# Scale column kept in idle norm columns; low parts of weight slots behind each quarter's sums; sums ahead of the odd chunk

## The reference: what is computed

```
c_act = jax.nn.silu(c)
mod = c_act @ ada_w[layer] + ada_b[layer]
sh_m, sc_m, g_m, sh_f, sc_f, g_f = jnp.split(mod, 6, axis=-1)
hm = x * (1.0 + sc_m) + sh_m
...
proj = (h @ w_in).astype(jnp.float32)
qa, ka, va, ra, aa, qkb, vb, ib, fb, ob = split_cols(proj, AB_SPLITS)
```

## Time and profile before

| | |
|---|---|
| median of 3 runs | 1407.68 us (1406.48 to 1409.59) |
| the profiled execution: its time, its span | 1406.98 us, 1405.2 us |
| mean granted TensorE clock | 0.981 |
| PE busy | 1343.3 us, 96% of the span |
| DVE, ACT, POOL busy | 619.5, 456.8, 507.5 us |

### The profile page before, as it was taken

One profiled execution on the slowest core, in us unless ns is written; L12 is line 12 of the kernel. 1 busy time (PEld: TensorE's weight loads), 2 busy tenths in 40 slices (PEclk: granted clock), 3 DMA queues, 4 the chain that ended last, 5 costly groups with the idle time before them and its releaser, 6 DMA issues.

```text
span 1405.2 us, 17072 instructions
## 1 busy us (share of the span) xinstructions
PE 1343.3 (96%) x6558; PEld 1111.4 (79%) x6558; DVE 619.5 (44%) x842; ACT 456.8 (33%) x622; POOL 507.5 (36%) x209
## 2 busy tenths in 40 slices
PE   7999999889999999999899999988989999999996
PEld 6778877778888888888788777878888888887885
DVE  4489657578534343300884323347692101100006
ACT  3343254333232332112322344316243323232112
POOL 0243222323453444344235122220254444444444
PEclk9999999999999999999999899999999999999998
DMA  9972546522555465643325421112023322234312
GB/s 332 165 150 80 190 135 121 180 76 98 191 190 195 163 218 173 183 129 96 119 80 191 113 90 53 42 57 76 30 91 108 101 91 103 90 103 137 90 60 60
DMA packets 93538, 173.81 MB, mean 124 GB/s; under 512 B 15736, under 2 KB 61960, under 8 KB 93357
## 3 DMA queue, kind: packets, MB, share of 16 engines
q1 hardware_dynamic: 90344, 169.63, 39.1%
q10 hardware_dynamic: 3140, 3.43, 0.9%
HBM read 170.87 MB, written 4.52 MB: 125 GB/s over the span
## 4 chain that ended last, share of the span: by engine, by line
PE 68%; issue 19%; POOL 6%; DVE 4%; ACT 1%; DMA 1%; SPq 0%; POOLq 0%; DVEq 0%; ACTq 0%
PE ps L1099 13%; PE ps L1100 13%; PE ps L1101 13%; POOL w_lo L692 6%; PE ps L1131 6%; PE ps L1132 6%; PE ps L1133 6%; PE ps L1614 1%; PE ps L1274 1%; PE ps L1275 1%; PE ps L1276 1%; PE ps L1642 1%; PE ps L1625 1%; PE ps L1629 1%; PE ps L1288 1%
## 5 line engine op out<-in xcount | busy, mean ns | idle before, releaser
L692 POOL TENSOR_TENSOR w_lo<-raw,w_hi 128x1024 fp32r<-128x1024 f32 x197 | 488.3, 2484 | 857.1 <-ACT w_hi L738 856.7
L1099 PE MATMUL ps<-h_lo,w_hi 128*128 128x512 f32 (+2 forms) x1064 | 402.0, 378 | 15.1 <-DVE h_lo L2138 5.9
L1100 PE MATMUL ps<-h_hi,w_hi 128*128 128x512 f32 (+2 forms) x1064 | 398.1, 374 | 0.0
L1101 PE MATMUL ps<-h_hi,w_lo 128*128 128x512 f32 (+2 forms) x1064 | 397.8, 374 | 0.0
L738 ACT ACTIVATE w_hi<-raw 128x1024 fp32r<-128x1024 f32 x203 | 213.2, 1057 | 483.9 <-PE ps L1133 177.0
L1099 PEld LDWEIGHTS ps<-h_lo,w_hi 128*128 128x128 f32 (+1 forms) x1064 | 203.8, 192 | 55.1 <-issue 8.4
L1101 PEld LDWEIGHTS ps<-h_hi,w_lo 128*128 128x128 f32 (+1 forms) x1064 | 203.7, 191 | 35.4
L1100 PEld LDWEIGHTS ps<-h_hi,w_hi 128*128 128x128 f32 (+1 forms) x1064 | 204.2, 192 | 34.2
L2235 DVE TENSOR_TENSOR tmp<-tmp,ps 128x512 f32<-128x512 f32 x44 | 30.1, 688 | 261.4 <-PE ps L1101 261.4
L1131 PE MATMUL ps<-w_hi,hid_lo 128*128 128x512 f32 x344 | 136.8, 398 | 1.8 <-issue 0.9
L1133 PE MATMUL ps<-w_lo,hid_hi 128*128 128x512 f32 x344 | 136.8, 398 | 0.0
(11 more groups left out here) (276 smaller groups left out, 1586.3 us busy)
## 6 DMA issues: line engine op xcount, KB each, us to landing
raw<-wstream SPq DMA_DIRECT2D x205, 512.0 KB, 4.0
ada_raw<-astream SPq DMA_DIRECT2D x80, 512.0 KB, 4.3
ada_first<-astream SPq DMA_DIRECT2D x16, 256.0 KB, 6.8
ada_first<-astream SPq DMA_DIRECT2D x8, 512.0 KB, 10.5
ln_rows<-row_scratch SPq DMA_DIRECT2D x3, 1024.0 KB, 6.7
skew_scratch<-f_scratch ACTq DMA_DIRECT2D x1, 2304.0 KB
xa<-xT SPq DMA_DIRECT2D x4, 512.0 KB, 8.5
out<-xa SPq DMA_DIRECT2D x3, 512.0 KB, 3.5
```

The lines of the kernel that those rows point to most:

```text
L692: nc.gpsimd.tensor_tensor(w_lo[:, slot, :], raw[:, slot % RAW, :], w_hi[:, slot, :].bitcast(F32), ALU.subtract).then_inc(sem("w_lo_ready"), 1)
L1099: pe.matmul(o, w_h, x_l, start=start, stop=False)
L1100: pe.matmul(o, w_h, x_h, start=False, stop=False)
L1101: return pe.matmul(o, w_l, x_h, start=False, stop=stop)
```

## The change

The place of `scale_b1` becomes the columns 0 to 7 of the sixth row of `cols`, which norms use only later; the arena begins 32 bytes lower. Row block 7 of quarter 3 goes from DVE to PE. On PE `first_cols(p + 1)` stands ahead of the odd chunk 2p + 1, for all three quarters that follow; before, it stood behind the first half of the odd chunk for p = 0 and 1, and ahead of chunk 5 for p = 2. On DVE, the low parts of slots 2, 3, 4 and 5 go behind all row blocks of the next quarter, and for p = 0 the low parts of chunk 0 and of slot 1 go ahead of the first row blocks of quarter 1.

```diff
-    scale_b1 = at("scale_b1", [P, KC])
...
+    scale_b1 = cols[:, 5, 0:KC]
...
-    FIRST_ON_PE = ((0, 1, 2, 3), (7,), (7,), ())
+    FIRST_ON_PE = ((0, 1, 2, 3), (7,), (7,), (7,))
...
         for p in range(4):
             for k in (2 * p, 2 * p + 1):
                 pe.wait_ge(sem("h_ready"), H_BASE["in"] + k + 1)
-                if k == 5:
-                    first_cols(3)
+                if k % 2 and p < 3:
+                    first_cols(p + 1)
                 for part in (first_qa, first_va) if k % 4 == 3 else (first_va, first_qa):
...
                     part(k)
-                    if k % 2 and p < 2 and part is (first_qa if k % 4 == 3 else first_va):
-                        first_cols(p + 1)
...
         for p in range(4):
             first_mod(p)
-            if p < 3:
+            if 1 <= p < 3:
                 first_block(p + 1, range(0, 2))
             lo_of_chunk(H_BASE["in"] + 2 * p, 2 * p)
             if p == 0:
                 first_lo(1)
+                first_block(1, range(0, 2))
             if p < 3:
                 first_block(p + 1, range(2, 3))
             lo_of_chunk(H_BASE["in"] + 2 * p + 1, 2 * p + 1)
             if p < 3:
-                first_block(p + 1, range(3, 5))
-                first_lo((2, 3, 5)[p])
-                first_block(p + 1, range(5, KC))
-            if p == 1:
-                first_lo(4)
+                first_block(p + 1, range(3, KC))
+            for s in ((2,), (3, 4), (5,), ())[p]:
+                first_lo(s)
```

More of the change, by code:

```diff
@@ L1865, in _ @@
         dve.wait_ge(sem("in_vec"), 16)
-        link(V.tensor_scalar(scale_b1[:], vec[:, V_ADAB + KC:V_ADAB + 2 * KC], 1.0, None, ALU.add))
+        link(V.tensor_scalar(scale_b1, vec[:, V_ADAB + KC:V_ADAB + 2 * KC], 1.0, None, ALU.add))
         dve.wait_ge(sem("c_ready"), 1)
```

## The result

| | time, us | ratio to before, 95% interval |
|---|---|---|
| before | 1408.47 (1406.48 to 1409.59, 4 runs) | |
| changed | 1400.29 (1398.94 to 1400.92, 4 runs) | 0.9938, 0.9925 to 0.9951 |

The change gains 8.2 us; I had forecast 3.9, about half of what came, and a range that ended at 1401.9. The direction was right, the size was not. The span of the profiled execution goes from 1405.2 to 1397.1.

What follows compares the result with a forecast made beforehand. The prediction took PE to bound the kernel; 1.33 + 1.23 + 2.13 - 0.83 = 3.86 us gained in the first stage gave a forecast of 1403.7 us, with an 8-in-10 range of 1401.9 to 1405.9.

Steps and rivals of the forecast that it cites:

- The start, 1.33: Chunk 0: DVE makes `h_lo` right behind the scale, so PE starts at 16.85 instead of 18.18, 1.33 us gained.
- The wait of quarter 1, 1.23: Before chunk 2: with sums earlier, 18 matmuls cover the way of 2.69 us; the wait goes, 1.23 us gained.
- of quarter 3, 2.13: Before chunk 5: PE no longer waits for DVE's last row blocks, 2.13 us gained.
- The slack of 0.6 for DVE's row blocks: Quarter 1: DVE ends its row blocks at 24.0, PE wants `ada_acc` at 24.6, so no wait.
- the upper bound of the gain: First stage: if slow matmuls end 1.3 us sooner than assumed, PE waits for DVE's 24.0; gain 4.5 us.
- Row block 7, 0.83 paid: Quarter 3: moving the block to PE makes its sums 1.71 us instead of 0.88, a cost of 0.83.
- Quarter 2's slack: Before chunk 4: added wait for slots 3 and 4 hidden by 0.6 us, the smallest slack; nothing gained.
- The sum of the stage, 3.86, bounds 3.2 to 4.5: First stage: PE through at 58.0 instead of 61.86, 3.86 us gained; clock bounds 3.2 to 4.5.
- The clock's scatter: PE's slow beginning: the number of slow matmuls differs by run, so the gain would scatter between 3.2 and 4.5 us.
- It arrives: Behind the first stage: the gain passes to the end; the rival, a transfer-bound supplier gives it back, 1407.7, had 8%.
- a clock rival: First stage: PE stays longer at the lower clock level, 32 more slow matmuls giving 1410.5; chance 3%.
- The storage, taken as nothing: Arena 32 bytes lower: weight loads of 189 against 192 ns, from nothing to 3 ns on 1032 loads, taken as 0.

Runs made afterwards that it cites:

- e6: Changed kernel with the sums on PE at their old place, keeping DVE's new order, storage and row block 7: 1399.55 us, ratio 0.994 to before.
- e7: Changed kernel with DVE's order of before, keeping the new place of the sums on PE, storage and row block 7: 1403.15 us, ratio 0.996 to before.
- e5: Changed kernel with row block 7 of quarter 3 summed by DVE again: 1398.58 us, ratio 0.9937 to before.
- e8: Changed kernel with twelve arena buffers of the first mixer moved up, eleven by 64 bytes and `neg_g` further: 1400.42 us, ratio 0.9939 to before.
- e2: Changed kernel with 32 unused bytes putting the arena back at its old place, new orders kept: 1403.97 us against 1408.04, ratio 0.9964.
- e12: The kernel before, unchanged, run for a second profile: one execution took 1409.84 us.
- e4: The changed kernel itself, run again: 1401.11 us, ratio 0.9952 to before.
- e1: The kernel before with the storage edit alone, all orders as before: 1403.3 us against 1408.04, ratio 0.9966.
- e3: Changed kernel with the arena 64 bytes up: 1403.84 us, ratio 0.9966 to before.
- e13: Changed kernel with all its buffers 64 bytes up together, so no distance changes: 1398.21 us against 1408.28, ratio 0.9937.
- e10: Changed kernel with `hid_lo` alone 32 bytes further up: one execution took 1405.45 us.

## Why the prediction was wrong, point by point

- **What bounds the kernel:** right for the first stage. I stopped at 242 us, though the storage edit touches what comes later.
- **The start, 1.33:** right. PE's idle time ahead of the first matmul fell from 3.88 to 2.55, in e6 as well. The starts themselves say 1.64 (18.18 to 16.54) and 1.1 (e6, 17.11), since the first scale comes at slightly different times in different executions.
- **The wait of quarter 1, 1.23, and of quarter 3, 2.13:** both gone. e6 and e7 show that the first needs both orders. The slack of 0.6 for DVE's row blocks was used up and 0.36 of wait came: DVE ended them as forecast (23.8, 24.0 forecast), but the lower level ended after 8 matmuls instead of 13, so PE came at 22.51 instead of 23.8. That is the case I had given as the upper bound of the gain.
- **Row block 7, 0.83 paid:** paid, but without it PE would have waited as long (e5). I booked it right in my sum, and named the wrong alternative: it is no cost of the change.
- **Quarter 2's slack:** held in this profile, by 0.2 us of the forecast 0.6 (`h_lo` of chunk 4 ends at 38.75, PE comes at 38.96). In e8's profile it did not: PE waited 0.47 there. It is the thin spot that I had called it.
- **The sum of the stage, 3.86, bounds 3.2 to 4.5:** 4.7 in the first profile by the starts, 4.4 from the first scale on, and 4.1 us by time in e2. Right, at the upper bound.
- **The clock's scatter:** the count of slow first matmuls does differ from run to run, 13 and 7 in the two profiles of before, 8 in the changed kernel's, 7 to 13 over all seventeen. The gain did not scatter with it: from the first scale to `narrow` the eleven profiles with all new orders take 42.9 to 43.8 us, the two of before 47.4 and 47.8. And I was wrong to take from one trace that the clock doesn't fall at 48.61; in e12 it did.
- **It arrives:** to 170 us whole; then 1.6 were lost to a lower clock, in e4 3.2. I had a clock rival, but for the start only. (The slack of slot 11 was 1.5, 85.7 less 84.2, not 1.4; nothing hangs on it.)
- **The storage, taken as nothing: the step that failed.** I bounded it by weight-load durations, 189 against 192 ns. They read 189 with the arena in either place, so that row can't show the cost. The distance between starts could, in the same trace of before: 0.2333 where `hid` is loaded (above), against 0.2267 (7.48 / 33) where `w` is loaded and `h` streams:

```profile
1150.05 0.39 PE L1100 MATMUL ps<-h_hi,w_hi 128*128 128x512 f32 x1
...
1157.53 0.39 PE L1100 MATMUL ps<-h_hi,w_hi 128*128 128x512 f32 x1
```

That difference was there to be asked about before any edit. In place of 0 stand 4.7 us by time (e1, interval 3.0 to 6.6) and 6.9 us of PE's time by the rows.

The Trainium skill, page "TensorE: Matmul & The Clock Gate", section "Part 2: What happens when you issue a matmul", says of SBUF's two read ports that loading the next weights doesn't take bandwidth from the running matmul. As I read it, the place of the loaded buffer should then not change a matmul's spacing. e3 and e13 differ from it: 0.2333 and 0.2267 us for the same matmuls, by distance alone. The measurement decides.

e5 and e13 measured a little under the changed kernel, but their intervals (0.9916 to 0.9958, 0.9919 to 0.9954) hold its 0.9938. No version is shown to beat it.

## What to carry to other kernels

An edit that moves storage by a few bytes is an edit to every instruction that reads behind it: look at the distance between starts of the long uniform streams, not at durations, before calling it free. Where weights are loaded beside a full stream of matmuls, keep the distance of loaded and streamed buffers at a multiple of 256 bytes (the best of the six remainders measured here, on this one kind of stream), and write an assertion for it. When sums and their consumers are joined by two engines, change both lists: here DVE's alone gave 3.0 us, PE's alone 1.0, both 4.3. And when a change is timed, look at the clock beside the time: here 11.3 us of work saved showed as 8.2.

## What was not expected of the hardware

- 512-column matmuls that load weights while they run start 0.2267 us apart when the streamed and the loaded buffer are a multiple of 256 bytes apart (215 and 192 times 256 here), and 0.2333 at the old distance. By beyond that multiple, summed over 1032 matmuls: 32 to 96 bytes cost 6.8 to 7.8 us, 128 bytes 5.8, 192 bytes 2.4. That it is a conflict of the two reads is my reading; the runs show only the distance.
- The matmul that runs while the misplaced weights are loaded pays most, not the one that uses them (e10: 138.3 us for line 1133, 134.8 for line 1131). Misplacing one load in three cost 6.1 us, misplacing all 6.9.
- A stretch of lower granted clock without a wait of PE ahead of it, at 170 us, came in 9 of 11 profiles of one order and in none of 6 of others, and gave back 1.6 to 3.2 us of the gain.
